# Order of the split products in the projections of a hybrid GLA, Mamba-2 and MoE layer

## The reference, cut to what matters

```python
h = rms_norm(x, norm1_g[l]) * (1.0 + sc1) + sh1
proj = h @ w_in[l]                              # 1024 x (q, k, v, g, gk, z, xbc, dt, gates)
q, k, v, g_out, gk_low, z, xbc, dt_raw, gates = split_cols(proj, IN_SIZES)
o_a = gla_mixer(q, k, v, g_out, gk_low, ...)    # 256 x 1024
o_b = ssd_mixer(z, xbc, dt_raw, ...)            # 256 x 2048
gate_a, gate_b = jnp.split(jax.nn.sigmoid(gates), N_BRANCH, axis=-1)
merged = gate_a * (o_a @ w_oa[l]) + gate_b * (o_b @ w_ob[l])
x = x + gt1 * (merged @ w_out[l])
h = rms_norm(x, norm2_g[l]) * (1.0 + sc2) + sh2
x = x + gt2 * hier_moe(h, ...)                  # 32 experts of width 256, top 2 of one group of 8
return rms_norm(x, final_norm_g)
```

## Time and profile before

| | |
|---|---|
| time, median of 3 runs | 701.45 us (700.1 to 701.8) |
| profiled execution, its time | 700.86 us |
| its span (first to last instruction) | 699.0 us |
| PE busy | 669.4 us (96%) |
| DVE busy | 420.1 us (60%) |
| ACT busy | 264.8 us (38%) |
| moved by DMA | 201.23 MB, mean 288 GB/s |

### The profile page before, as it was taken

The page is one execution under the profiler, slowest core; times in us unless marked ns, Lnnn a source line. Parts: engine busy times, 40 slices in busy tenths (PEclk is TensorE's granted clock), DMA queues, the critical chain, the costliest instruction groups (busy, mean ns, idle before and its releaser), DMA issues.

```text
span 699.0 us, 12784 instructions
## 1 busy us (share of the span) xinstructions
PE 669.4 (96%) x5402; PEld 538.5 (77%) x5402; DVE 420.1 (60%) x710; ACT 264.8 (38%) x373; POOL 71.4 (10%) x70
## 2 busy tenths in 40 slices
PE   8999999999999999999998999899999999999893
PEld 8999999998777777999988997675666666665441
DVE  4656788987866789977786678644333122221226
ACT  3346545557763624335552332312131121221003
POOL 0001000000003614300000000001112111111111
PEclk9999999999999999999999999999999999999998
DMA  8987764455343443346639976999999999999992
GB/s 363 423 353 243 298 248 175 130 177 191 121 157 130 161 142 121 122 140 253 241 108 397 410 280 249 423 421 418 419 397 418 421 421 421 419 418 418 420 355 95
DMA packets 31195, 201.23 MB, mean 288 GB/s; under 512 B 5047, under 2 KB 5431, under 8 KB 7970
## 3 DMA queue, kind: packets, MB, share of 16 engines
q1 hardware_dynamic: 27378, 193.27, 70.7%
q0 software_dynamic: 3760, 7.14, 2.8%
HBM read 195.35 MB, written 10.75 MB: 295 GB/s over the span
## 4 chain that ended last, share of the span: by engine, by line
PE 77%; DVE 9%; DMA 6%; ACT 3%; issue 2%; SPq 2%; DVEq 0%; POOL 0%; ACTq 0%; POOLq 0%
PE ps L1571 75%; DMA ring<-in_expert_pieces 4%; DVE ring_rounded L934 2%; DMA ring<-in_pieces 2%; ACT ring_rounded L644 2%; SPq L461 1%; PE ps L1988 1%; PE ps L1692 1%; DVE r_ct L1209 1%; DVE r_v L1209 1%; DVE r_xs_rounded L1239 1%; ACT sq L760 1%; DVE g_sb L1142 0%; DVE r_kq L1173 0%; DVE newton L920 0%
## 5 line engine op out<-in xcount | busy, mean ns | idle before, releaser
L934 DVE TENSOR_TENSOR ring_rounded<-ring,ring_rounded 128x2048 fp32r<-128x2048 f32 x60 | 136.8, 2291 | 38.8 <-ACT ring_rounded L644 38.5
L1571 PE MATMUL ps<-hT_rounded,ring_rounded 128*128 128x256 f32 x832 | 150.1, 286 | 1.1 <-ACT hT_rounded L658 1.1
L1571 PEld LDWEIGHTS ps<-hT_rounded,ring_rounded 128*128 128x128 f32 x832 | 129.2, 193 | 5.1 <-issue 3.9
L644 ACT CAST ring_rounded<-ring 128x2048 fp32r<-128x2048 f32 x60 | 114.1, 1906 | 34.4 <-PE ps L1571 18.8
L1571 PE MATMUL ps<-ring_rounded,hT_rounded 128*128 128x512 f32 x352 | 109.7, 393 | 0.9 <-DVE ring_rounded L934 0.9
L1571 PE MATMUL ps<-x_sb_rounded,ring_rounded 128*128 128x256 f32 x416 | 109.8, 284 | 0.0
L1571 PEld LDWEIGHTS ps<-x_sb_rounded,ring_rounded 128*128 128x128 f32 x416 | 77.3, 193 | 0.9 <-issue 0.2
L1571 PEld LDWEIGHTS ps<-ring_rounded,hT_rounded 128*128 128x128 f32 x352 | 64.3, 188 | 14.8 <-issue 1.4
L858 ACT ACTIVATE sq<-ps 128x128 f32<-128x128 f32 x32 | 8.9, 277 | 142.6 <-PE ps L1571 142.6
L1454 DVE TENSOR_TENSOR r_st<-ps,r_kq 128x512 f32<-128x512 f32 x32 | 22.1, 692 | 65.0 <-PE ps L1571 65.0
L603 POOL DMA_INDIRECT y_rows<-r_st,r_btm x29 | 28.5, 984 | 311.4 <-DVE r_st L1454 298.6
(11 more groups left out here) (336 smaller groups left out, 1002.9 us busy)
## 6 DMA issues: line engine op xcount, KB each, us to landing
ring<-in_pieces SPq DMA_DIRECT2D x66, 1024.0 KB, 5.0
ring<-in_expert_pieces SPq DMA_DIRECT2D x48, 1024.0 KB, 17.5
r_z<-in_expert_pieces SPq DMA_DIRECT2D x12, 1024.0 KB, 13.3
r_xs<-in_expert_pieces SPq DMA_DIRECT2D x12, 1024.0 KB, 12.5
r_v<-in_pieces SPq DMA_DIRECT2D x6, 1024.0 KB, 7.2
r_ct<-in_pieces SPq DMA_DIRECT2D x6, 1024.0 KB, 5.6
g_sb<-in_expert_pieces SPq DMA_DIRECT2D x6, 1024.0 KB, 17.2
r_st<-in_expert_pieces SPq DMA_DIRECT2D x6, 1024.0 KB, 17.9
```

The lines of the kernel that those rows point to most:

```text
L644: nc.scalar.copy(high_of(p_), slot_of(p_)).then_inc(hi_ok, 1)
L934: nc.vector.tensor_tensor(low_of(p_), slot_of(p_), high_of(p_).bitcast(F32), ALU.subtract).then_inc(lo_ok, 1)
L1571: return nc.tensor.matmul(o, l, r, start=start, stop=stop)
```

## The change

The low products of a piece come after all its high products. TensorE waits for the high part first, and for the low part only ahead of the low products. In a channel-major half both column blocks are summed at once in their bank, and in `ob` all products of one row piece are done before the next. In the first half of a token-major unit the high products of both token tiles come before the low ones of both; in the second half each tile is finished in turn. The sums have the same terms in another order.

```diff
-            def split_product(o, l, r, start, stop):
-
-                for n_, (a_, b_) in enumerate(((0, 0), (0, 1), (1, 0))):
-                    ins = mm(o, l[a_], r[b_], start and n_ == 0, stop and n_ == 2)
-                return ins
-
-            def parts(p_):
+            def high_ready(p_):
+                pe.wait_ge(hi_ok, SPLIT_AT[p_] + 1)
+                return high_of(p_)
+
+            def low_ready(p_):
                 pe.wait_ge(lo_ok, SPLIT_AT[p_] + 1)
-                return high_of(p_), low_of(p_)
+                return low_of(p_)
...
-                    for a in range(2):
-                        for r in range(n_r):
-                            w = parts((*u, half, r))
+                    for r in range(n_r):
+                        p_ = (*u, half, r)
+                        w = high_ready(p_)
+                        for a in range(2):
                             for k in range(KD):
-                                ins = split_product(bank[:, a * T:(a + 1) * T], [v[:, k, a * P:(a + 1) * P] for v in w],
-                                                    [v[:, r * KD + k] for v in src], r == 0 and k == 0,
-                                                    r == n_r - 1 and k == KD - 1)
-                            if a == 1:
-                                ins.then_inc(done if r == n_r - 1 else ob_read, 1)
+                                for part in src:
+                                    mm(bank[:, a * T:(a + 1) * T], w[:, k, a * P:(a + 1) * P], part[:, r * KD + k],
+                                       r == 0 and a == 0 and k == 0 and part is src[0], False)
+                        w = low_ready(p_)
+                        for a in range(2):
+                            for k in range(KD):
+                                ins = mm(bank[:, a * T:(a + 1) * T], w[:, k, a * P:(a + 1) * P], src[0][:, r * KD + k], False,
+                                         r == n_r - 1 and a == 1 and k == KD - 1)
+                        ins.then_inc(done if r == n_r - 1 else ob_read, 1)
...
+                    def with_high(t):
+                        w = by_rows(high_ready(p_))
+                        bank = bank_of(u, t)[0]
                         for kh in range(KD // 2):
                             k = half * KD // 2 + kh
                             if u == ("out", 0) and t == 0 and k % 2 == 0:
                                 merged(k)
-                            ins = split_product(bank[:], [v[:, k, t * P:(t + 1) * P] for v in src], [v[:, kh] for v in w],
-                                                k == 0, k == KD - 1)
+                            for part in src:
+                                mm(bank[:], part[:, k, t * P:(t + 1) * P], w[:, kh], k == 0 and part is src[0], False)
+
+                    def with_low(t):
+                        w = by_rows(low_ready(p_))
+                        bank, done = bank_of(u, t)
+                        for kh in range(KD // 2):
+                            k = half * KD // 2 + kh
+                            ins = mm(bank[:], src[0][:, k, t * P:(t + 1) * P], w[:, kh], False, k == KD - 1)
                         if half:
                             ins.then_inc(done, 1)
                         elif t:
                             ins.then_inc(half_read, 1)
+
+                    if half:
+                        for t in range(TT):
+                            with_high(t)
+                            with_low(t)
+                    else:
+                        for t in range(TT):
+                            with_high(t)
+                        for t in range(TT):
+                            with_low(t)
```

More of the change, by code:

```diff
@@ L1661, in token_major @@
                 for half in range(2):
-                    w = [v.rearrange("p a b -> p (a b)").rearrange("p (k n) -> p k n", n=CW) for v in parts((*u, half, 0))]
-                    for t in range(TT):
-                        bank, done = bank_of(u, t)
+                    p_ = (*u, half, 0)
+                    by_rows = lambda v: v.rearrange("p a b -> p (a b)").rearrange("p (k n) -> p k n", n=CW)
+                    def with_high(t):
+                        w = by_rows(high_ready(p_))
+                        bank = bank_of(u, t)[0]
                         for kh in range(KD // 2):
```

## The result

The changed kernel takes 693.3 us (median of four executions, 692.3 to 694.0) where the kernel before takes 701.1 beside it (four, 700.1 to 701.8): a ratio of 0.989, 95% interval 0.9875 to 0.991, or 7.8 us. In a second comparison, made later, the same two kernels stand at 694.9 and 700.2 us (6 and 23 executions), ratio 0.992 (0.990 to 0.994), or 5.3 us. The profiled execution of after has a span of 691.7 us against 699.0.

A forecast was written before the change was run, and what follows sets the result against it. TensorE holds 77% of the chain, but the expert stream, released after VectorE's last modulation row (L1209), sets the end. Gains of 0.9 (z wait) and 4.6 (ob wait) sum to 5.5 us: 695.9 us forecast, range 694.0 to 699.5.

The forecast's parts named there:

- the ob wait: In the second half of ("ob", 0), at 385 us: TensorE gains 4.9 us, of which 4.6 reach VectorE's L1209.
- TensorE's two waits: TensorE's waits for low parts (L934), ahead of the third z block and in ("ob", 0), 4.1 us together, go.
- Pace costed at 0: Regrouping matmuls into high and low passes costs 0 in all weight pieces; bounds 0 and +39.7 us.
- The z wait, 0.9 us: Ahead of the third z block, at 244 us: the low part is needed later, gain 0.9 us, bounds 0 and 0.9.
- Added waits at 0: In the token-major halves: 100 more waits cost 0; at 55 ns each they would use up the gain.
- the stream's start sets the end: Expert weight loads, begun by SP after VectorE's L1209, set the end; starting 5.5 us earlier ends the kernel 5.5 us earlier.
- the stream would hide most of a late fall of the clock: After TensorE's wait for L1287: a clock drop costs out's last blocks up to 1.5 us, mostly hidden by expert loads.
- speeding TensorE beside it is worth nothing: Beside the expert weight stream: what only speeds TensorE up does not bring the end forward.
- The clock fell elsewhere: Rival, at TensorE's wait for L1287 ahead of 438.46 us: clock drop loses up to 1.5 us, 697.4 us; chance 0.06.
- Landing takes over: Rival, in ob: an awaited piece lands 2.5 us later, the sum shrinks to 3.0 us, 698.4 us; chance 0.18.
- Nothing: Rival, expert stream: slots rather than bandwidth set its pace and the lead is lost by 665 us, 701 us; chance 0.09.
- slower: Rival, between 512-column matmuls: 100 added waits at 100 ns cost 10 us against 5.5 gained, 705.9 us; chance 0.07.

The follow-up runs named there:

- e12: The changed kernel with 800 more already satisfied waits, ten ahead of each of the 80 token-major passes; 694.4 us.
- e1: The kernel before with the new order in the two ob units alone; 3.1 us gained on the kernel before, at 699.7 us beside it.
- e15: The changed kernel with twelve satisfied waits ahead of each token-major half, 192 ahead of ob; one execution, landing 17.86 us after the issue, no wait in ob.
- e8: The kernel before with five satisfied waits ahead of each half of v, g, z and out, 80 ahead of ob; ratio 0.998.
- e13: The kernel before with two satisfied waits ahead of each half of v, g, z and out, 32 ahead of ob; one execution, late landing and full ob wait.
- second pair: A second profiled execution of the kernel before and of the changed kernel, both unchanged; difference -4.7 us.
- e10: The changed kernel with two gate rows (2 MiB) loaded ahead of SP's wait for modulation row 9; time can't be told from the changed kernel.
- e5: The kernel before, unchanged, in a second profiled execution; the 3.2 us ob wait came again.
- e14: The kernel before with ten satisfied waits ahead of each half of v, g, z and out, 160 ahead of ob; one execution, landing 17.43 us after the issue.

## Why the prediction was right in kind and short in size

The time lies below the range through two steps: the ob wait was put at too little, and the range had no width for a slow clock in the start that one execution has and the next has not.

*TensorE's two waits (right).* Both are gone, and so is the slow clock in ob. *Pace costed at 0 (right).* 106.42 and 106.41 us for the same stretch in the two kernels. *The z wait, 0.9 us (right).* S1-S2 fell by 1.1 and 1.0 us. *Added waits at 0 (right).* e12; the 100 waits became 60 instructions. The Trainium skill's 50 to 100 ns for reading a semaphore (page Advanced Engine Details and Errata, section Network/Comms) gave an estimated 5 to 10 us more; no run here shows that price in a stream of matmuls.

*The step that was mis-sized: the ob wait, 4.6 us, on a landing held fixed.* The prediction left the awaited piece at 381.44 us and let VectorE's L1209 win 4.6 of TensorE's 4.9. Measured: S2-S3 lost 5.2 us in the first pair and 6.2 in the second, and from the first matmul of ob to the first of out TensorE went from 51.2 to 46.1 us, 5.1 instead of 4.9. e1, which has the new ob and the late landing, gives 4.5: the prediction's own term, with its own premise. The other 0.7 us goes with the piece landing 1.3 us earlier, in the new order wanted by VectorE rather than by TensorE; e15, the changed kernel with the late landing, puts it lower, at 0.4 (54.1 against 53.7). e8 and e13, which move no product, tie that to where the added waits of TensorE's program put its instruction load. The second pair's further 1.0 us is a slow clock of 6.8 us instead of 3.4 at the same wait in the kernel before.

*The term that was put at nothing without a reason: the start, 1.8 us.* The sum was made against one execution, in which the clock also fell near 61 us with TensorE busy. The window would have shown it (0.67, 26 matmuls in 4 us). It comes in six of seventeen profiled executions, in either kernel, so it was a width for the range, and the range had none for it. Without that column the change is worth 5.5 us in the first pair and 6.5 in the second. That the first is the sum's 5.5 to the tenth is luck: the ob wait gave 0.6 us more, the z wait 0.2 and the stretch from the router on 0.8, and a late fall of the clock, which the kernel before had only in its second profile, took 1.6 back.

*The step that failed in kind but cost little: the stream's start sets the end.* L1209 does gate SP, as said, but it also stands ahead of VectorE's residual sums, which gate TensorE's way to the router, and that is the consumer that counts (e10). Both hang on the same instruction, so the sum was not hurt. Two of its conclusions were: that the stream would hide most of a late fall of the clock, and that speeding TensorE beside it is worth nothing.

*The rivals.* The clock fell elsewhere, at the place that the rival named, and took 1.6 us from S3-S4 in the first pair; but it falls there in e5, e8, e13 and e14 too, whose ob is the old one. So the new order of ob doesn't cause it. "Landing takes over" went the other way: the piece came 1.3 us earlier behind the issue, not 2.5 later. "Nothing" and "slower" are ruled out by the ratio and by e12. The Trainium skill, page TensorE: Matmul & The Clock Gate, section Why this matters for your kernels, has idle gaps drop the clock. The trace agrees for the falls in ob and at the router, not for the one at 61 us, and several waits of the same length had no fall behind them.

## What to carry to other kernels

When a piece of weights is prepared in two steps, put the products that need the second step last over as much work as the open accumulators allow; here that took away a wait of 3.2 us and left TensorE 1.8 us to spare even with the late landing (e1, e15). Before a sum is made against one profiled execution, look through all its windows for a slow clock outside the stage in question, and widen the range by each. And when two engines are released by the same instruction, find out which of them the end follows before calling the other free.

## What the runs showed of the hardware that was not expected

The clock fell for 3.4 us near 61 us with TensorE busy for the whole of it, in six of seventeen executions, at a cost of about 1.7 us each (180.7 to 180.8 us up to S1 against 179.1 on average). Behind waits the length did not decide: it fell after waits of 1.6, 1.8, 2.0 and 2.2 us and did not after others of 1.9, 2.2, 2.4 and, in e14, 2.9 us. It fell for 3.4 us or for 6.8 at waits of the same 3.2 us.

An instruction load of 16 KB, 1 us of one DMA engine, goes with later landings when it falls into a list of 1 MB loads: from the first landing behind it on (in e13 from the second), each comes 0.7 to 1.5 us late (e5, e13, e14, e15; 0.2 to 0.4 in e12). Lengthening one engine's program by 80 waits moved it out, and the kernel's median was 1.5 us lower (ratio 0.998, 0.997 to 1.000, at the edge of what was measured). 800 satisfied waits in a stream of matmuls cost no time, though the trace records most of their instructions with 0.05 us each.
